# Branch products in three one-pass terms, and gates finished on VectorE

## The reference

```
proj = rmsnorm(x) @ w_in                          # q, k, v of 24 heads, and 3 x 1024 gate columns
gates = sigmoid(proj[..., 3 * MIX_WIDTH:])        # three gates of 1024
o_a = dilated_mixture(q, k, v)                    # 12 heads folded into 4 outputs: 256 wide
o_b = moba_attention(q, k, v)                     # 6 heads: 384 wide
o_c = stick_breaking_attention(q, k, v)           # 6 heads: 384 wide
merged = gates[0] * (o_a @ w_out_a) + gates[1] * (o_b @ w_out_b) + gates[2] * (o_c @ w_out_c)
x = x + merged @ w_o
x = x + square(relu(rmsnorm(x) @ w_up)) @ w_down
```

## Time and profile before

| | |
|---|---|
| median of 3 runs | 1977.03 (1976.48 to 1983.36) |
| profiled execution | 1986.21, span 1984.4 |
| mean granted TensorE clock | 0.98 |
| TensorE busy | 1908.5 (96%), 15280 matmuls |
| VectorE / ScalarE / POOL busy | 880.9 (44%) / 960.8 (48%) / 1362.3 (69%) |
| chain that ended last | 88% TensorE, 4% VectorE, 3% ScalarE, 1% POOL |
| y, both layers | 256 pass records of L1140, 380 ns each, overlapping |

### The profile page before, as it was taken

The page is one execution under the profiler, slowest core; times in us unless marked ns, Lnnn a source line. Parts: engine busy times, 40 slices in busy tenths (PEclk is TensorE's granted clock), DMA queues, the critical chain, the costliest instruction groups (busy, mean ns, idle before and its releaser), DMA issues.

```text
span 1984.4 us, 36368 instructions
## 1 busy us (share of the span) xinstructions
PE 1908.5 (96%) x15280; PEld 1836.0 (93%) x15280; DVE 880.9 (44%) x1785; ACT 960.8 (48%) x1491; POOL 1362.3 (69%) x628
## 2 busy tenths in 40 slices
PE   6999997999999999889999999999999999999999
PEld 3999995899999998869999998989999999999999
DVE  3675587374137578745121633143311623243322
ACT  2544455344454445444444445646544445646543
POOL 0888770388878887316888865537897865537896
PEclk8999998999999999989999999999999999999999
DMA  9999650595579896317555653436664643346662
GB/s 317 357 347 310 223 191 23 196 367 191 175 268 367 300 304 189 106 44 270 189 161 169 210 168 119 137 122 198 194 210 149 212 149 128 128 147 192 194 204 94
DMA packets 357075, 397.90 MB, mean 201 GB/s; under 512 B 9016, under 2 KB 319024, under 8 KB 356912
## 3 DMA queue, kind: packets, MB, share of 16 engines
q1 hardware_dynamic: 356752, 395.38, 60.1%
q10 hardware_dynamic: 160, 0.20, 0.0%
HBM read 394.51 MB, written 1.05 MB: 199 GB/s over the span
## 4 chain that ended last, share of the span: by engine, by line
PE 88%; DVE 4%; ACT 3%; POOL 1%; SPq 1%; issue 1%; DMA 1%; DVEq 0%; ACTq 0%
PE bank L717 75%; PE bank L803 3%; PE bank L1140 2%; POOL w_lo L683 1%; PE bank L934 1%; PE bank L974 1%; SPq L545 1%; PE bank L748 1%; PE bank L752 1%; PE bank L749 1%; DVE arena L1776 1%; PE bank L708 1%; ACT arena L1353 1%; DVE bank L1703 1%; DMA arena<-in_ada_w 1%
## 5 line engine op out<-in xcount | busy, mean ns | idle before, releaser
L683 POOL TENSOR_TENSOR w_lo<-ring,w_hi 128x1024 fp32r<-128x1024 f32 (+2 forms) x624 | 1362.1, 2210 | 607.2 <-ACT w_hi L1217 606.5
L1217 ACT ACTIVATE w_hi<-ring 128x1024 fp32r<-128x1024 f32 (+2 forms) x624 | 595.2, 978 | 408.0 <-PE bank L717 370.7
L717 PE MATMUL bank<-hn,w_hi 128*128 128x256 f32 x2752 | 774.6, 281 | 4.0 <-POOL w_lo L683 3.0
L717 PE MATMUL bank<-hn_lo,w_hi 128*128 128x256 f32 x2752 | 766.9, 279 | 0.0
L717 PE MATMUL bank<-hn,w_lo 128*128 128x256 f32 x2752 | 766.9, 279 | 0.0
L717 PEld LDWEIGHTS bank<-hn,w_hi 128*128 128x128 f32 x2752 | 519.5, 189 | 8.0 <-POOL w_lo L683 4.8
L717 PEld LDWEIGHTS bank<-hn_lo,w_hi 128*128 128x128 f32 x2752 | 519.2, 189 | 1.1 <-issue 0.5
L717 PEld LDWEIGHTS bank<-hn,w_lo 128*128 128x128 f32 x2752 | 519.6, 189 | 0.0
L717 PE MATMUL bank<-gated,w_hi 128*128 128x256 f32 x1408 | 247.2, 280 | 0.0
L717 PEld LDWEIGHTS bank<-gated,w_hi 128*128 128x128 f32 x1408 | 215.2, 189 | 0.0
L717 PE MATMUL bank<-gated,w_lo 128*128 128x256 f32 x704 | 197.2, 280 | 0.0
(11 more groups left out here) (219 smaller groups left out, 2332.2 us busy)
## 6 DMA issues: line engine op xcount, KB each, us to landing
ring<-in_ffn_w_in SPq DMA_DIRECT2D x88, 1024.0 KB, 7.4
ring<-in_w_in SPq DMA_DIRECT2D x72, 1024.0 KB, 5.1
arena<-in_ada_w SPq DMA_DIRECT2D x35, 2048.0 KB, 10.6
ring<-in_w_up SPq DMA_DIRECT2D x32, 1024.0 KB, 5.4
ring<-in_w_down SPq DMA_DIRECT2D x32, 1024.0 KB, 5.1
ring<-in_ffn_w_out SPq DMA_DIRECT2D x32, 768.0 KB, 4.8
ring<-in_ffn_w_out SPq DMA_DIRECT2D x32, 640.0 KB, 4.1
ring<-in_w_in SPq DMA_DIRECT2D x16, 512.0 KB, 3.6
```

The source lines that it names most:

```text
L683: pool.tensor_tensor(w_lo[:, q, ks], ring[:, r, k0:k0 + n], w_hi[:, q, ks], ALU.subtract) \
L717: last = mm(out, a, b, start=start and i == 0, stop=stop and i == 2)
L1217: f(w_hi[:, q, half * 4:half * 4 + n], ring[:, r, k0:k0 + n], ACT.Copy).then_inc(weights_rounded, 1)
```

## The change

- Block two's y is multiplied in three one-pass terms: its weight chunks join the rounding by ScalarE and the splitting by POOL, and `pair_out` writes a head pair as two rounded parts (o2_hi, then o2_lo = bank - o2_hi).
- The gates leave the bank as exp(-z) instead of z. VectorE adds 1 (and caps the sum at 3e38) and takes the reciprocal, 512 columns at a time, in the heads' loop: unit p's gate at the end of the step after the one that copied it, the last after the loop. The sigmoids and their two changes of table go.
- ScalarE rounds y0 at the end of step 16 and y1 at the end of step 18, y2 and y3 around "merged hi 0"; wo0 and wo1 follow one merged chunk later than before.
- merged_parts lies elsewhere in the arena.

```diff
-for _part, _phases in (..., ("two", ("z2", "wo", "up", "dn"))):
+for _part, _phases in (..., ("two", ("z2", "y", "wo", "up", "dn"))):
...
-        o2 = view(18432, KT, S)
-        merged, merged_parts = view(9216, KT, S), rounded("merged_parts", 0, 2, KT, S)
+        o2_hi, o2_lo = rounded("o2_hi", 18432, KT, S), rounded("o2_lo", 0, KT, S)
+        merged, merged_parts = view(9216, KT, S), rounded("merged_parts", 2048, 2, KT, S)
...
-                    pe.wait_ge(weights_in[s], eng.arrived("y", i))
+                    half_ready("y", i, 0)
...
-                            for k in range(nk):
-                                last = mm(b[:, c], ring[:, s, k0 + k, c * P:(c + 1) * P], o2[:, k0 + k, :],
-                                          start=(k == 0), stop=(k == nk - 1))
+                            for k in range(k0, k0 + nk):
+                                if c == 0 and k == 4:
+                                    half_ready("y", i, 1)
+                                last = terms(b[:, c], w_hi[:, q, k, ws], w_lo[:, q, k, ws], o2_hi[:, k], o2_lo[:, k],
+                                             False, k == k0, k == k0 + nk - 1)
+                                if c == 1 and k == 3:
+                                    last.then_inc(weights_used, eng.step(f"half used y {i}", weights_used))
...
-                    f(dst, b, ACT.Copy).then_inc(scalar_done, eng.step(f"z2 out {i}"))
+                        f(gates[:, 2 * (i - 18):2 * (i - 17), :], b, ACT.Exp, scale=-1.0) \
+                            .then_inc(scalar_done, eng.step(f"z2 out {i}"))
...
+                    if i == len(Z2_BETWEEN) - 3:
+                        round_chunk("y", 0)
+                    if i == len(Z2_BETWEEN) - 1:
+                        round_chunk("y", 1)
...
-                functions("sigmoid_and_others")
-                for i in range(4):
-                    if i == 2:
-                        act.wait_ge(scalar_done, eng.at("z2 out 29"))
-                    for br in range(3):
-                        g = gates[:, 8 * br + 2 * i:8 * br + 2 * i + 2, :]
-                        f(g, g, ACT.Sigmoid).then_inc(scalar_done, eng.step(f"gate {i}" if br == 2 else None))
-                    if i == 2:
-                        merged_hi(0)
-                functions(ln_exp)
+                round_chunk("y", 2)
+                merged_hi(0)
+                round_chunk("y", 3)
+                merged_hi(1)
                 round_chunk("wo", 0)
-                merged_hi(1)
+                merged_hi(2)
                 round_chunk("wo", 1)
-                merged_hi(2)
                 merged_hi(3)
...
+                hi, lo = dst(hd)
+                dve.tensor_copy(hi, b).then_inc(vector_done, eng.step())
+                dve.wait_ge(vector_done, eng.at())
+                tt(lo, b, hi, ALU.subtract).then_inc(vector_done, eng.step(mark))
...
+                def gate(p):
+                    u = Z2_UNITS[p][0]
+                    g = gates[:, 2 * (u - 18):2 * (u - 17), :]
+                    dve.wait_ge(scalar_done, eng.at(f"z2 out {u}"))
+                    ts(g, g, 1.0, 3e38, ALU.add, ALU.min).then_inc(vector_done, eng.step())
+                    dve.wait_ge(vector_done, eng.at())
+                    dve.reciprocal(g, g).then_inc(vector_done, eng.step())
+                def gates_of(i):
+                    for p, half in Z2_BETWEEN[i]:
+                        if half == 1 and Z2_UNITS[p][0] >= 18:
+                            gate(p)
+                attention(HEADS_TWO, tile2, lambda hd: (o2_hi[:, hd.out_tile, :], o2_lo[:, hd.out_tile, :]),
+                          lambda i: gates_of(i - 1) if i else None)
+                gates_of(len(Z2_BETWEEN) - 1)
+                dve.wait_ge(vector_done, eng.at())
```

More of the change, by code:

```diff
@@ L215 @@
 SPLIT_START, SPLIT_CHUNKS = {}, {}
-for _part, _phases in (("one", ("f1in", "f1out", "z", "f2in", "f2out")), ("two", ("z2", "wo", "up", "dn"))):
+for _part, _phases in (("one", ("f1in", "f1out", "z", "f2in", "f2out")), ("two", ("z2", "y", "wo", "up", "dn"))):
     _at = 0
@@ L690, in _ @@
             for layer in eng.layers("two"):
-                for phase in ("z2", "wo", "up", "dn"):
+                for phase in ("z2", "y", "wo", "up", "dn"):
                     for i in range(TWO[phase]):
@@ L1126, in _ @@
                 for i in range(4):
-                    s = slot_of("y", i)
-                    pe.wait_ge(weights_in[s], eng.arrived("y", i))
+                    q = split_slot("y", i)
+                    half_ready("y", i, 0)
                     if i == 0:
@@ L1138, in _ @@
                         for c in range(2):
-                            for k in range(nk):
-                                last = mm(b[:, c], ring[:, s, k0 + k, c * P:(c + 1) * P], o2[:, k0 + k, :],
-                                          start=(k == 0), stop=(k == nk - 1))
+                            ws = slice(c * P, (c + 1) * P)
+                            for k in range(k0, k0 + nk):
[5 more added lines that the diff above has]
+                                    last.then_inc(weights_used, eng.step(f"half used y {i}", weights_used))
                         if br == 1:
                             last.then_inc(tensor_done, eng.step(f"y {i}"))
-                    last.then_inc(weights_free[s], 1)
+                    last.then_inc(weights_used, eng.step(f"used y {i}", weights_used))
                 for i in range(4):
@@ L1504, in copy_out @@
                         dst = v2[:, :, 256 * (i - 12):256 * (i - 11)]
-                    else:
-                        dst = gates[:, 2 * (i - 18):2 * (i - 17), :]
-                    f(dst, b, ACT.Copy).then_inc(scalar_done, eng.step(f"z2 out {i}"))
+                    if i < 18:
+                        f(dst, b, ACT.Copy).then_inc(scalar_done, eng.step(f"z2 out {i}"))
+                    else:
+                        f(gates[:, 2 * (i - 18):2 * (i - 17), :], b, ACT.Exp, scale=-1.0) \
+                            .then_inc(scalar_done, eng.step(f"z2 out {i}"))
                 for p in range(BEFORE_HEADS):
@@ L1828, in pair_out @@
                 dve.wait_ge(tensor_done, eng.at(f"out {hd.name}"))
-                dve.tensor_copy(dst(hd), bank[:, 6 + hd.pair % 2, 0:S]) \
-                    .then_inc(vector_done, eng.step(f"heads {heads[0].name} {hd.pair}"))
+                b, mark = bank[:, 6 + hd.pair % 2, 0:S], f"heads {heads[0].name} {hd.pair}"
+                if heads is HEADS_ONE:
+                    dve.tensor_copy(dst(hd), b).then_inc(vector_done, eng.step(mark))
+                    return
+                hi, lo = dst(hd)
+                dve.tensor_copy(hi, b).then_inc(vector_done, eng.step())
+                dve.wait_ge(vector_done, eng.at())
+                tt(lo, b, hi, ALU.subtract).then_inc(vector_done, eng.step(mark))
             tap = [0]
@@ L2058, in _ @@
                     dve.wait_ge(vector_done, eng.at())
-                attention(HEADS_TWO, tile2, lambda hd: o2[:, hd.out_tile, :], lambda i: None)
+                def gate(p):
[13 more added lines that the diff above has]
+                dve.wait_ge(vector_done, eng.at())
                 for i in range(4):
                     dve.wait_ge(tensor_done, eng.at(f"y {i}"))
-                    dve.wait_ge(scalar_done, eng.at(f"gate {i}"))
                     dst = merged[:, 2 * i:2 * i + 2, :]
@@ L2067, in _ @@
                         if br == 2:
-                            dve.wait_ge(weights_free[slot_of("y", i)], eng.freed("y", i))
+                            dve.wait_ge(weights_used, eng.at(f"used y {i}"))
                         b = bank[:, 3 * (i % 2) + br].rearrange("p (c s) -> p c s", c=2)
```

## The result

The changed kernel takes 1.0123 times the time of the kernel before (95% interval 1.0096 to 1.0151), 24 us more on 1977, or about 2001. A second set of runs gave 1.0112 (1.0074 to 1.0150), 22 us. Single executions of the changed kernel lay between 1992 and 2010; the medians of the two sets are 2007 and 1998. It is slower, as forecast.

The account below looks back on a forecast made before the run. TensorE, busy 96%, and VectorE's merging were taken to bound the kernel closely together. Heads 2 x 8.5 plus 7.8 after them gave +24.8, or +19.6 at the low end; +23 on 1977 made 2000, range 1979 to 2007.

Parts of the forecast that it names:

- TensorE's saving of 5.8 a layer hidden by the merging: Branch products: one-pass terms take 22.0 instead of 27.82, but VectorE's merging, slower than TensorE, sets the end.
- Merging period 7.37: VectorE's merging of a chunk takes 7.37, its adds held by POOL's splits, against TensorE's 5.5.
- End of the heads: Last gate delays merged 0 to T + 12.65 (11.85 if its tensor_scalar precedes POOL): both layers together +7.8 (6.2).
- The reciprocal: VectorE's gates: a 128x512 reciprocal grows with its columns and takes 3.7 to 4.2, taken as 4.0.
- Stalls of the heads: Gates between a head pair's copy and the next maxima make TensorE wait: 8.5 a layer at a 4.0 reciprocal.
- 3.3 + 0.5 and 4.7: TensorE's stalls per layer: 3.3 from step 5, some 0.5 from the late maxima of steps 7 and 8, 4.7 from step 8.
- The low value of the range: Heads' stalls of 6.7 a layer with a 3.7 reciprocal; with 6.2 after the heads, +19.6 in all.
- Which steps: In the heads, gates stall TensorE from steps 5 and 8, which also copy a head pair; other steps have room.
- (a): Rival, chance 0.10: the reciprocal takes 0.69, a gate 1.2; branch products end +0.3 and +0.9 later, time 1978.
- (b): Rival, chance 0.09: the reciprocal is slow but the heads absorb it; only the part after them costs, +8, 1985.
- (c): Rival, chance 0.06: VectorE's adds escape POOL's splits, a chunk merges in 5.04; -6.4 and -5.9, time 1965.
- (d): Rival, chance 0.05: a long reciprocal and POOL exclude each other in the heads: +20 more, time 2020.

Follow-up runs that it names:

- the products alone: Kernel before with three-term branch products only, gates still by ScalarE's sigmoid: 1.0039 of the kernel before.
- the sum in a bank: Changed kernel with each chunk's merged sum built in a PSUM bank instead of SBUF: 1.0004 of the kernel before.
- the gates only: Kernel before with gates as exponentials finished by VectorE's reciprocals in the heads, branch products plain: 1.0082 of the kernel before.
- half the reciprocal: Changed kernel without the reciprocal for 256 of each gate's 512 columns: 1.0039 of the kernel before.

## Why the prediction was right, and where it was not

The time, 2000 forecast and 2001 measured, and both mechanisms (a long reciprocal that holds up the maxima in the heads, and a merging held by POOL's splits) were right; some terms under them were not, and that the sum came out within 1 us is partly luck: the measured interval alone spans 19 to 30.

- **TensorE's saving of 5.8 a layer hidden by the merging.** Right: the products alone won nothing. Once the adds no longer waited it came out whole, 6.8 and 6.7.
- **Merging period 7.37.** Measured 7.40 to 7.43. Its cause, two SBUF operands against POOL's split, is shown by the sum in a bank.
- **End of the heads.** Of the two orders, the tensor_scalar got in ahead of POOL (0.42). Merged 0 came at T + 11.6 for 11.85, the last tiles at T + 35.4 for 35.4: +2.8 and +3.4, the forecast's lower value of 6.2. Of the reciprocal's 0.65 less than assumed only 0.25 came through, because the adds that follow end with POOL's splits (2.67 and 2.05 for 0.69).
- **The reciprocal.** Taken at 4.0 from a range of 3.7 to 4.2, measured 3.35: below the range. From two to 512 columns it grows by (3353 - 159) / 510 = 6.3 ns a column; the difference between means of 157 and 173 over two columns was too coarse for a factor of 255. The Trainium skill's "VectorE: DVE Perf Modes", section "First, the fixed hardware budget" (repeat count of 8), read as eight cycles an element, gave an estimate of 4.4, further off still. The choice between 0.69 and about 4 was what mattered.
- **Stalls of the heads.** 8.5 a layer forecast, 8.6 and 8.3 measured, but this sum is right partly by chance. The waits are 2.4 and 2.6 in layer 0, 2.4 and 3.6 in layer 1, and not 3.3 + 0.5 and 4.7. The gate is 0.65 shorter at both places (by the forecast's own steps that leaves 7.2 a layer), the 0.5 did not show, and in layer 0 the second tensor_scalar took 0.66 and not 1.5. The maxima start 3.7 after their scores in step 6, and not over 4. In place of what is missing, TensorE's lower clock after the wait costs 1.9 and 1.8 in layer 0 and 1.8 in layer 1; I had no such term.
- **The low value of the range.** 6.7 a layer for a reciprocal of 3.7 can't be redone from the steps given; with each stall 0.3 shorter it would be 7.9, and the low end of the sum some 22 and not 19.6.
- **Which steps.** Steps 5 and 8 alone, as forecast: with the gate before the copy, which changes the order in just those steps as far as the maxima are concerned, the heads are back at 86.5.
- **Rivals.** (a) falls with 3.35; (b) with the heads' 95.1; (c) with adds of 1.8 to 2.7. (d) falls too. Timelines of VectorE and POOL, changed kernel:

```profile
1225.87 3.35 DVE L2077 RECIPROCAL arena<-arena 128x512 f32<-128x512 f32 x1
```

```profile
1226.89 4.70 POOL L683 TENSOR_TENSOR w_lo<-ring,w_hi 128x1024 fp32r<-128x1024 f32 x2 [7.34 <-ACT w_hi L1222]
```

POOL starts within the reciprocal and takes its usual 4.70 for two splits. The rule in the Trainium skill's "SBUF — State Buffer", section "SBUF: two separate sides", agrees with the adds (up to 2.67 for 0.69) and the tensor_scalars here (1.63 for 0.42); the reciprocal behaves as an operation outside it.

The second wait differs between the layers (2.6 and 3.6) through the clock of the first. VectorE's timeline has the second gate's tensor_scalar in layer 0, then in layer 1:

```profile
1245.21 0.66 DVE L2075 TENSOR_SCALAR arena<-arena 128x512 f32<-128x512 f32 x1
...
1700.76 1.63 DVE L2075 TENSOR_SCALAR arena<-arena 128x512 f32<-128x512 f32 x1
```

In layer 0 the first unit ran at the lower clock (7.39), so TensorE reached step 8's outputs later and the gate met only the end of POOL's split; in layer 1 it ran at 1.00 (5.71), and the gate met more of it. No run varied this on purpose, but the sum in a bank, the gates only and half the reciprocal go the same way: 0.46 to 1.11 after a slow first unit, 1.42 and 1.43 after a fast one.

Open: when the clock falls. The length of the wait alone doesn't decide it. In layer 1 of the run with the sum in a bank both waits are 2.4; these are the first 3 us after each:

```profile
1678.30:1681.30 3.00, 3.00 (x14) 3.00 (x15) 2.93 (x7) 0.79 (x3) 2.15 (x1) 0.50 0.00 0
1703.20:1706.20 3.00, 2.96 (x25) 2.99 (x26) 2.00 (x4) 2.72 (x4) 3.00 (x2) 1.00 0.00 0
```

## What to carry to other kernels

Work given to an engine with idle time is free only inside its waits: put it ahead of the instruction on which that engine waits anyway, not between that wait and what others are waiting for, and follow the queues (here maxima, exponentials, rounding, split, product) to the engine that sets the time. Where two chains end within a microsecond of one another, shortening one wins nothing; look for what bounds the second, here an SBUF operand that could stand in PSUM, and change both. And price an operation that the trace doesn't show at its own size before giving it a place.

## What the runs showed of the hardware

- VectorE's reciprocal on float32 takes 3.35 for 512 columns and 1.75 for 256, 6.3 ns a column, where a multiplication of 512 columns takes 0.69 and a tensor_scalar from SBUF to SBUF 0.42. It and POOL's tensor_tensor run beside each other without delay (3.35 and 4.70 for two splits).
- Across the changed kernel, the sum in a bank and the gates only, TensorE waited twelve times in the heads for 1.9 to 3.6, at a granted clock of 0.98 to 1.00 up to the next unit. After ten of these waits the clock read 0.50 to 0.73 in the next 3 us, and the z2 unit took 1.6 to 2.0 longer; after two, both of 2.4, it stayed at 1.00. So it did after the four waits of 0.8 to 1.6 with half the reciprocal. Where the clock fell, it added half to all of the wait's length again. In the changed kernel's merging it fell as well (0.50 from 1327 to 1333, after 2.9 without work), at no cost, since TensorE doesn't set the pace there.
- An fp32 add that reads its running sum from PSUM costs 0.70, the same as from SBUF, and never waited for POOL, which was busy beside it.
